# Channel mixers of a decoder trunk by Strassen's seven products, with 'up' and 'down' as separate phases

## What is computed

```python
def squared_relu_mlp(h, w1, w2):          # the channel mixer: w1 1024 x 4096, w2 4096 x 1024
    return square(relu(h @ w1)) @ w2

for i in range(2):
    h = rms_norm(x, norm_mix_pre[i])
    m = chunked_gmlp(h, ...) if i == 0 else stick_breaking_attention(h, ...)
    x = x + rms_norm(m, norm_mix_post[i])
    h = rms_norm(x, norm_ffn_pre[i])
    f = squared_relu_mlp(h, mlp_w1[i], mlp_w2[i])
    x = x + rms_norm(f, norm_ffn_post[i])
```

## Time and profile before

| | us |
|---|---|
| median of 3 runs | 2825.63 |
| lowest, highest | 2821.26, 2829.11 |
| span of the profiled execution | 2821.4 |
| PE busy in it | 2682.1 |
| DVE, ACT, POOL busy | 1196.0, 826.6, 714.8 |

### The profile page before, as it was taken

One profiled execution on the slowest core, in us unless ns is written; L12 is line 12 of the kernel. 1 busy time (PEld: TensorE's weight loads), 2 busy tenths in 40 slices (PEclk: granted clock), 3 DMA queues, 4 the chain that ended last, 5 costly groups with the idle time before them and its releaser, 6 DMA issues.

```text
span 2821.4 us, 36750 instructions
## 1 busy us (share of the span) xinstructions
PE 2682.1 (95%) x13772; PEld 2272.5 (81%) x13772; DVE 1196.0 (42%) x1607; ACT 826.6 (29%) x1243; POOL 714.8 (25%) x372
## 2 busy tenths in 40 slices
PE   7998999899999999999999988888989999999998
PEld 7997777777888888887898867667888888888886
DVE  3216666665333433334511135555253334334344
ACT  4223122134122121122301257777242221211212
POOL 2222121122222222223322244444132222222222
PEclk9999999999999999999999999999999999999999
DMA  4222121133111111113323553342131111111122
GB/s 157 90 89 90 60 66 54 59 112 97 47 58 45 45 45 59 45 45 112 128 90 134 176 159 90 97 106 72 61 114 51 60 46 45 45 59 45 45 82 105
DMA packets 112145, 224.51 MB, mean 80 GB/s; under 512 B 9536, under 2 KB 76096, under 8 KB 110016
## 3 DMA queue, kind: packets, MB, share of 16 engines
q1 hardware_dynamic: 105408, 194.02, 22.1%
q10 hardware_dynamic: 6656, 29.36, 2.6%
HBM read 177.23 MB, written 46.14 MB: 79 GB/s over the span
## 4 chain that ended last, share of the span: by engine, by line
issue 44%; PE 35%; POOL 10%; DVE 7%; ACT 4%; DMA 1%; POOLq 0%; DVEq 0%; ACTq 0%; SPq 0%
PE psum L578 12%; PE psum L565 9%; POOL w_lo L505 9%; PE psum L589 6%; PE psum L821 3%; DVE stick L1401 2%; PE psum L791 2%; PE psum L808 2%; DVE vst L1253 2%; ACT psum L1105 1%; PE psum L667 1%; ACT brk L1099 1%; POOL xt L520 1%; DVE vn_lo L1262 1%; ACT vn_hi L997 1%
## 5 line engine op out<-in xcount | busy, mean ns | idle before, releaser
L505 POOL TENSOR_TENSOR w_lo<-stage,w_hi 128x1024 fp32r<-128x1024 f32 x208 | 500.8, 2428 | 1815.7 <-ACT w_hi L876 1815.7
L565 PE MATMUL psum<-hT_hi,w_hi 128*128 128x512 f32 x1536 | 599.0, 390 | 2.0 <-POOL w_lo L505 2.0
L565 PE MATMUL psum<-hT_lo,w_hi 128*128 128x512 f32 x1536 | 598.5, 390 | 0.0
L565 PE MATMUL psum<-hT_hi,w_lo 128*128 128x512 f32 x1536 | 598.2, 389 | 0.0
L589 PE MATMUL psum<-w_hi,a_hi 128*128 128x512 f32 x1280 | 504.3, 394 | 25.9 <-DVE acc L1247 16.6
L1247 DVE TENSOR_TENSOR acc<-psum,acc 128x512 f32<-128x512 f32 x544 | 373.6, 691 | 317.0 <-PE psum L589 313.5
L589 PE MATMUL psum<-w_lo,a_hi 128*128 128x512 f32 x1280 | 502.3, 392 | 0.0
L589 PE MATMUL psum<-w_hi,a_lo 128*128 128x512 f32 x1280 | 502.2, 392 | 0.0
L876 ACT ACTIVATE w_hi<-stage 128x2048 fp32r<-128x2048 f32 x104 | 198.8, 1911 | 812.5 <-PE psum L589 665.8
L565 PEld LDWEIGHTS psum<-hT_hi,w_hi 128*128 128x128 f32 x1536 | 288.9, 188 | 62.2 <-issue 2.0
L565 PEld LDWEIGHTS psum<-hT_hi,w_lo 128*128 128x128 f32 x1536 | 288.7, 188 | 60.3
(11 more groups left out here) (88 smaller groups left out, 2622.5 us busy)
## 6 DMA issues: line engine op xcount, KB each, us to landing
stage<-mlp_w_in SPq DMA_DIRECT2D x64, 1024.0 KB, 5.3
stage<-a_w_in_in SPq DMA_DIRECT2D x16, 1024.0 KB, 5.5
x_res<-xt SPq DMA_DIRECT2D x24, 512.0 KB, 4.9
xt<-x_res SPq DMA_DIRECT2D x24, 512.0 KB, 5.2
stage<-b_w_qkv_in SPq DMA_DIRECT2D x12, 1024.0 KB, 5.1
xt<-x_in SPq DMA_DIRECT2D x16, 512.0 KB, 4.3
v_gelu<-vring ACTq DMA_DIRECT2D x8, 1024.0 KB, 3.9
vst<-v_gelu SPq DMA_DIRECT2D x8, 1024.0 KB, 4.8
```

The lines of the kernel that those rows point to most:

```text
L505: pool.tensor_tensor(wt[b][1][:, c], stage[:, c], wt[b][0][:, c].bitcast(F32), ALU.subtract).then_inc(unit_ready, 1)
L565: mm = pe.matmul(psum[:, bank, :], wt[ub][sw][:, k * UC + f * P:k * UC + (f + 1) * P], hT[sh][:, k, half * HALF:(half + 1) * HALF], start= ...
```

## The change

For both mixers the products are cut in halves in all three dimensions and formed by Strassen's seven products of half size, in the variant with shared sums. 'Up' becomes a phase of its own: for each of 16 chunks (two blocks of 128 hidden columns, one from each half) seven products (c, p) of 12 matmuls, into PSUM chains A, B and C of two sets of banks (`UP_BANK`). Some of the seven are accumulated on one another in a bank, others are copied out by ACT (`e_buf`) and added by DVE. The seven forms of the input (`H[layer][p]`: sums and differences of its quarters, hi and lo) are made once per mixer, in the turn, from 28 transposed 128x512 blocks (`quad`; `QUADS`) and sums on POOL and DVE (`h_forms`). The weights' forms (`S`) are sums by DVE (POOL for chunk 0), split by ACT and POOL per product. Squares go to `a_out`, DVE makes the forms of the activations (`a_form`), and SP stores all seven to DRAM (`a_dram`), 1.84 MB a chunk.

'Down' is a second phase of 28 steps (4 units of 4 chunks x 7 products): SP loads an activation form (1 MB) and, 4 of 7 times, a block of w2 (1 MB); ACT and POOL split the weights, ACT and DVE the activations, into a ring of three; DVE makes four weight forms per unit (`block_form`); each step is four products of 12 matmuls, and after each DVE adds the bank into `acc` or copies it. The last four steps run interleaved by pairs of tiles (`down_order`).

The loops of the mixers are written out in full. Buffers lie on top of each other anew, so the weights of the v, q and k products go through other buffers (`stage_q`, `wq`), and the first two units of the attention's output weights are loaded and split inside the first round of the attention instead of before it.

The core of the diff (whole functions that only rename buffers, the definitions of tiles and semaphores, and the removed mixer code are left out):

```diff
+def up_order():
+    seq = [(0, 1), (0, 2), (1, 1), (1, 2), (0, 5), (0, 6), (0, 3), (0, 7),
+           (1, 5), (0, 4), (1, 6), (1, 3), (1, 7)]
+    for c in range(2, CH_M):
+        seq += [(c, 1), (c, 5), (c - 1, 4), (c, 6), (c, 3), (c, 2), (c, 7)]
+    return seq + [(CH_M - 1, 4)]
...
+CHAIN = {1: "A", 6: "A", 7: "A", 4: "A", 5: "C", 3: "C", 2: "B"}
...
+def down_order():
+    seq = [(n, tp) for n in range(STEPS - 4) for tp in range(HALF_T)]
+    for a, b in ((STEPS - 4, STEPS - 3), (STEPS - 2, STEPS - 1)):
+        for g in (0, 2):
+            seq += [(a, g), (a, g + 1), (b, g), (b, g + 1)]
+    return seq
...
+def down_bank(n, tp):
+    return tp + (4 if DOWN_P[n % 7] in (5, 3, 2) else 0)
...
+def finishes(t):
+    after = {0: DOWN_AT[(STEPS - 4, 0)], 1: DOWN_AT[(STEPS - 3, 1)], 2: DOWN_AT[(STEPS - 4, 2)], 3: DOWN_AT[(STEPS - 3, 3)],
+             4: DOWN_AT[(STEPS - 2, 0)], 5: DOWN_AT[(STEPS - 1, 1)], 6: DOWN_AT[(STEPS - 2, 2)], 7: DOWN_AT[(STEPS - 1, 3)]}
+    return range(after[t], after[t + 1] if t < NT - 1 else DOWN_N)
...
+            def load_up(layer, c):
+                if c >= 2:
+                    sp.wait_ge(up_lo, max(up_ready(layer, c - 2, p) for p in range(1, 8)))
+                if c % 2 == 0:
...
+            def mlp_loads(layer):
+                load_up(layer, 2)
+                for c in range(1, CH_M):
...
+                    store_a(layer, c - 1, 0)
+                    if c + 2 < CH_M:
+                        load_up(layer, c + 2)
+                    if c == CH_M - 1:
+                        load_block(layer, 0, "11")
+                        load_a(layer, 0)
+                        load_a(layer, 1)
+                        load_block(layer, 0, "22")
+                        load_block(layer, 0, "12")
+                    store_a(layer, c, 1)
+                    store_a(layer, c, 2)
+                load_block(layer, 0, "21")
+                store_a(layer, CH_M - 1, 0)
+                for n in range(2, STEPS):
...
+                        load_block(layer, v + 1, {3: "11", 4: "22", 5: "21", 6: "12"}[j])
+                    if n == STEPS - 4:
+                        sp.wait_ge(up_out, OUT_N * (layer + 1))
+                        load_g(2 * layer + 2)
+                        for t in range(4):
+                            load_x(2 * layer + 2, t)
...
+            sp.wait_ge(front_psum, FI_O)
+            unit(U_O, cols(w_bout, 0), stage_c)
...
+            def mlp_boundary(b, layer):
+                w_forms(layer)
+                if layer:
+                    up_split(layer, 0, 1)
+                    up_split(layer, 0, 2)
+                add_x(b)
+                h_forms(b, layer, 0)
+                if not layer:
+                    up_split(layer, 0, 1)
+                    up_split(layer, 0, 2)
+                h_forms(b, layer, 1)
+                up_split(layer, 1, 1)
+                up_split(layer, 1, 2)
+                w_forms_rest(b, layer)
+                for c, p in UP[4:]:
+                    up_split(layer, c, p)
+                for n in range(STEPS - 1):
+                    down_w_split(layer, n)
...
+            mlp_boundary(1, 0)
+            add_x(2, 0, 2)
+            down_w_split(0, STEPS - 1)
+            add_x(2, 2)
+            lo_units(U_V2, U_O, wq, stage_q)
...
+            def up_product(layer, c, p):
+                pe.wait_ge(up_lo, up_ready(layer, c, p))
+                if p in (6, 3, 7):
+                    pe.wait_ge(up_copy, COPY_N * layer + COPY_AT[(c, {6: 1, 3: 5, 7: 6}[p])] + 1)
+                elif p == 4:
+                    pe.wait_ge(up_sum, SUM_N * layer + SUM_AT[(c, 7)] + 1)
+                elif c >= 2:
+                    pe.wait_ge(up_out, OUT_N * layer + OUT_AT[(c - 2, {1: 4, 2: 2, 5: 3}[p])] + 1)
+                bank = UP_BANK[c % 2][CHAIN[p]]
...
+            def mlp_up(b, layer):
+                pe.wait_ge(quad_lo, QUAD_N * layer + NT)
+                up_product(layer, 0, 1)
+                up_product(layer, 0, 2)
+                if layer == 0:
+                    pe.wait_ge(back_evac, BI_END)
+                for p in (5, 6, 3, 7, 4):
+                    quad(b, layer, p, 0)
+                up_product(layer, 1, 1)
+                for p in (5, 6, 3, 7, 4):
+                    quad(b, layer, p, 1)
+                up_product(layer, 1, 2)
+                for p, i in QUADS[NT + 10:]:
+                    quad(b, layer, p, i)
+                for c, p in UP[4:]:
+                    if c == 0 and p in (5, 6, 3, 7):
+                        pe.wait_ge(quad_lo, QUAD_N * layer + QUAD_AT[(p, 3)] + 1)
+                    elif (c, p) == (1, 5):
+                        pe.wait_ge(quad_lo, QUAD_N * (layer + 1))
+                    up_product(layer, c, p)
...
+            def down_product(layer, n, tp):
+                at_ = STEPS * layer + n + 1
+                if tp == 0:
+                    pe.wait_ge(down_w_lo, at_)
+                    pe.wait_ge(down_a_lo, at_)
+                before = down_before((n, tp), down_bank)
+                if before is not None:
+                    pe.wait_ge(down_acc, DOWN_N * layer + before + 1)
+                else:
...
+            def mlp_down(layer, turn):
+                for n, tp in DOWN:
+                    down_product(layer, n, tp)
+                    if turn:
...
+            def down_take(layer, n):
+                g, v, p = STEPS * layer + n, layer * UNITS + n // 7, DOWN_P[n % 7]
...
+            def mlp(b, layer):
...
+                    if p in (1, 5, 6):
+                        up_copy_out(layer, c, p)
+                    while n >= 4 and taken < UP_N and UP_AT.get((UP[taken][0] - 1, UP[taken][1]), 0) <= n:
+                        up_take(layer, *UP[taken])
+                        taken += 1
+                    if p in (3, 2, 7, 4):
+                        up_relu_out(layer, c, p)
+                    if (c, p) == (CH_M - 1, 2):
+                        down_take(layer, 0)
+                    if (c, p) == (CH_M - 1, 4):
+                        down_take(layer, 1)
+                for n in range(2, STEPS - 1):
+                    down_take(layer, n)
...
+                    if first and n in (2, 4):
+                        hi(U_O + n // 2 - 1, n // 2 - 1)
...
+                    if 3 <= t <= 6:
+                        quad_split(layer, 1, t - 3)
+                        quad_split(layer, 2, t - 3)
+                pre_norm(b, NT - 2)
+                for p in (5, 6, 3, 7, 4):
+                    quad_split(layer, p, 0)
+                pre_norm(b, NT - 1)
+                h_forms(b, layer, 2)
+                for p in (5, 6, 3, 7, 4):
+                    quad_split(layer, p, 1)
+                h_forms(b, layer, 3)
+                for p, i in QUADS[NT + 10:]:
+                    quad_split(layer, p, i)
...
+            def mlp(b, layer):
+                for c, p in LEAVE:
+                    if p in (3, 2, 7):
...
+                        forms = {5: (1,), 6: (2,), 3: (4,), 7: (3,)}.get(p, ())
+                    else:
+                        forms = {1: (1,), 5: (2,), 6: (4,), 3: (3,)}.get(p, ())
+                    if c + 1 < CH_M:
+                        for s in forms:
+                            w_form(layer, c + 1, s)
+                    if p == 7:
+                        a_form(layer, c, 3)
+                    if p in (3, 2, 7, 4):
+                        up_square_out(layer, b, c, p)
+                    if p == 7:
+                        a_form(layer, c, 1)
+                        a_form(layer, c, 2)
+                    if p == 4:
+                        a_form(layer, c, 4)
+                    if (c, p) == (CH_M - 1, 2):
+                        for k in range(KU):
+                            down_split(layer, 0, k)
+                block_form(layer, 0, 1)
+                for k in range(KU):
+                    down_split(layer, 1, k)
+                block_form(layer, 0, 2)
+                for n in range(STEPS - 4):
+                    v, j = n // 7, n % 7
+                    if j in (0, 1):
+                        block_form(layer, v, 3 + j)
+                    elif j in (5, 6) and v + 1 < UNITS:
+                        block_form(layer, v + 1, j - 4)
+                    for tp in range(HALF_T):
+                        down_add(layer, n, tp)
+                        if n + 2 < STEPS:
+                            down_split(layer, n + 2, tp)
+                for k in range(KU):
+                    down_split(layer, STEPS - 2, k)
+            def finish_down(layer):
                 def finish(t):
-                    for n2 in range(2):
-                        ins = accumulate(False, bi + 2 * t + n2, 2 * t + n2, per)
-                        ins.then_inc(back_evac, 1)
+                    for k in finishes(t):
+                        down_add(layer, *DOWN[k])
+                    if t == 2:
```

889 lines of the change are left out of this document (627 added, 262 removed).

## The result

The changed kernel takes 2764.8 us (median of four runs, 2760.6 to 2768.7) where the kernel before takes 2825.9: a ratio of 0.978, 95% interval 0.977 to 0.980. That is 61 us gained, where 88 were forecast. The profiled execution of after has a span of 2758.8 us against 2821.4, so 62.6 us are to be accounted for.

What follows compares the result with a forecast made beforehand. Inside the mixers PE's matmul count at 226.6 ns each was taken as the bound, DVE at the turns. Span 2821.4 - 174.0 + 34 + 22 + 16 + 4 + 5 + 5 = 2733.4, plus 4.2: 2738 us; range 2695 to 2795.

Steps and rivals of the forecast that it cites:

- matmuls removed: In both mixers, 768 fewer matmuls at 0.2266 us each: 174.0 us saved.
- steady 'up' and 'down': Inside both phases PE stays busy and single late steps are absorbed: 5 us cost, bounds 0 and 30.
- turns into the mixers: Before each mixer, transposed blocks and sums on DVE delay PE: 17 us each, 34 us, bounds 20 and 56.
- 'up' to 'down': Between the phases, PE waits for late activations, last square and weights: 11 us each, 22 us, bounds 10 and 36.
- behind mixer 0: After mixer 0, tiles finishing in pairs and later next weights stall PE: 16 us, bounds 5 and 22.
- end of the kernel: In the last 'down' steps, 3 us of stall and 1 of tail: 4 us, bounds 1 and 8.
- attention: Splits of two output weight units on ACT and POOL inside the first round: 5 us, bounds 0 and 13.4.
- the five places: PE waits only twice at the turns' blocks, twice between 'up' and 'down', and in the last four steps.
- Rival 1: In 'down', the resource shared by POOL and DVE decides: 55 us more, 2793 us; chance 0.15.
- Rival 3: In 'up', late loads behind a wait on SP's queue make it slower than before, 2933 us; chance 0.05.
- Rival 2: The turns cost half because gaps overlap: 86 becomes 45 us, 2697 us; chance 0.15.
- rival 4: A gap of 0.2 us at each of 448 product ends costs 90 us: 2828 us; chance 0.03.

Runs made afterwards that it cites:

- Experiment 1: Changed kernel with the load of the third attention output weight unit moved behind the loop over later head pairs on SP's queue: 2750.7 us against 2764.8.
- two passes: Changed kernel with one of the three passes of every 'down' product left out, all else kept, output less exact: 2733.6 us against 2764.8.

## Why the prediction was right or wrong

The sign, the range (2695 to 2795) and the mechanism held; the forecast of 2738 was 27 us too low. That it came no further off is in part luck: attention, the transitions and the turns cost 36 us more than forecast, while the stretch behind mixer 0 and the steady parts cost 13 less. By its own terms, forecast and then measured in the trace, in us:

```
                          forecast   measured
matmuls removed            -174.0     -174
steady 'up' and 'down'         +5        0
turns into the mixers         +34      +40.1  (19.7, 20.4)
'up' to 'down'                +22      +36.1  (17.7, 18.4)
behind mixer 0                +16       +8.3
end of the kernel              +4       +6.5
attention                      +5      +20.6
q, k and v                      0       -0.2
sum                         -88.0      -62.6
```

The two lines "behind mixer 0" and "end" are what remains of 45.7 and 45.3 us when the measured turn and transition are taken off.

- **Attention is the step that failed.** The forecast counted what the splits cost ScalarE and POOL in the first round, and not what the moved load meets on SP: the load waits for a split in the round, and the loads of the second head pair stand behind it. Its bounds, 0 to 13.4, had only the two engines in them, and attention was not among the five places where waits of PE were due. Experiment 1 gives 11.5 us of the 20.6 back within attention.
- **'Up' to 'down' was right in kind, too small in size**: the same chain was named (form loaded late, ScalarE, four differences, sum), and its wait forecast at 6.5 us was 7.2 and 6.1; the one for the last square, laid at 2.8, was 1.5 in both. The second step's weights, "a good 1 us late", were 4.5 and 4.9 late, since POOL's four splits took 10.5 us beside VectorE and not 4.8, and the clock was 0.66 and 0.83 behind the waits. What remained for both, 36.1, lies just above the term's upper bound of 36.
- **The turns** came within 3.4 us each. The products behind the last blocks, forecast for about 684, start at 686.9 in mixer 0 (the forecast's own list adds up to 684.8). What it left out is that sums of VectorE take 1.7 us beside POOL's instead of 0.69, and the clock, 3.4 us in the first turn.
- **Behind mixer 0** the two stalls laid out (5.5 and 3.9) came as one of 6.0 us before the transposes and one of 0.6; POOL's wait was 8.5, forecast 10. At the end of the kernel the stall was 4.9 where 3 was laid out: the differences of step 27 (5.8 us beside POOL) stand before the add that PE waits for.

```profile
2717.84 5.78 DVE L1953 TENSOR_TENSOR ra_lo<-a_raw,ra_hi 128x512 fp32r<-128x512 f32 x4
```

- **Steady parts: PE bound**, as said, and the 5 us there were not needed.
- **Rival 1** (the shared resource decides in 'down') did not come to pass, but two passes show by how little: a step needs 10.0 us without TensorE as its bound, 0.9 below the 10.9 that it has. The forecast's own count, 10.3 in the heavy steps, was near this. The Trainium skill, "SBUF — State Buffer", "Who interferes with whom", says that the two contend for a shared port pair, as an exclusive lock; the trace agrees in that both kinds grow (684 to 1031 ns, 1.1 to 1.5 us) and adds of PSUM do not.
- **Rival 3** (late loads in 'up') had no sign in the waits, and the half-size loads in 512-byte pieces landed, two issued together, as fast as a whole one (median us from issue to landing):

```profile
stage<-mlp_w_in SPq DMA_DIRECT2D x16, 1024.0 KB, 6.0
raw<-mlp_w_in SPq DMA_DIRECT2D x32, 512.0 KB, 5.8
```

By the Trainium skill, "DMA: Bandwidth & Descriptors", Specifications (512 B still at line rate), that was due, and this trace agrees. Rival 2 (turns at half price) and rival 4 (gaps at product ends) fell with the windows above: the turns cost more, and a matmul still starts each 226.2 ns.

## What to carry to other kernels

When a change moves a load into another stage, list what stands behind it in the same queue and when the buffer that it waits for becomes free; its bytes and its engines' time say nothing on that. A product saved inside a stage where PE is never idle brings its full price, as the 226.2 ns a matmul show; what comes back comes back at the seams, where one late supplier costs its wait and, in the two places measured here, about a third as much again, mostly in clock. Reordering a seam pays only after every queue that meets there has been read: of the reorders run here two gained clear of the spread of the runs (14 and 7 us), one shows 4 us in its own stretch, and the others moved the wait or made a new one.
